# A two-layer hybrid decoder trunk: reciprocal roots of the norms on DVE alone, and the norm weights applied where the high and low parts are made

## The reference

```python
def rmsnorm(x, g):
    xf = x.astype(jnp.float32)
    y = xf * lax.rsqrt(jnp.mean(xf * xf, axis=-1, keepdims=True) + EPS)
    return (y * g.astype(jnp.float32)).astype(x.dtype)

def reference(x, mem, ...):
    for l in range(DEPTH):
        h = rmsnorm(x, norm_mix[l])
        qa, ka, va, qb, kb, vb, qi, ki, wi, qc, kc, vc, g = _split(h @ w_in[l], IN_SIZES)
        o_a = stick_breaking_attention(...)
        o_b = dsa_attention(rmsnorm(qb, qn_dsa[l]), rmsnorm(kb, kn_dsa[l]), vb, ...)   # top 64 keys
        o_c = sliding_window_attention(rmsnorm(qc, qn_swa[l]), rmsnorm(kc, kn_swa[l]), vc, ...)
        gates = jax.nn.sigmoid(g + b_gate[l])
        merged = gates[0] * (o_a @ w_pa[l]) + gates[1] * (o_b @ w_pb[l]) + gates[2] * (o_c @ w_pc[l])
        x = x + merged @ w_out[l]
        x = x + cross_attention(rmsnorm(x, norm_x[l]), rmsnorm(mem, norm_mem[l]), ...)
        hf = rmsnorm(x, norm_ffn[l])
        if l % 2 == 0:
            x = x + swiglu(hf, w_gu_dense[l // 2], w_down_dense[l // 2])
        else:
            x = x + moe_swiglu(hf, w_router[l // 2], w_gu_moe[l // 2], w_down_moe[l // 2])   # 2 of 8 experts
    return x
```

## Time and profile before

| what | value |
|---|---|
| time, median of 3 runs | 1813.37 us (1812.16 to 1819.61) |
| the profiled execution's own time | 1814.6 us |
| its span | 1813.0 us |
| mean granted PE clock | 0.984 of full |
| PE busy | 1717.1 us (95%) |
| DVE busy | 1405.6 us (78%) |
| ACT busy | 1112.3 us (61%) |
| POOL busy | 93.7 us (5%) |

### The profile page before, as it was taken

How to read it: one execution, slowest core, us unless ns; L and a number is a source line. 1 busy time by engine, 2 the same in 40 slices (tenths; PEclk the granted TensorE clock), 3 DMA queues, 4 the chain that set the end, 5 groups by cost and what they waited for, 6 DMA issues and landing times.

```text
span 1813.0 us, 22257 instructions
## 1 busy us (share of the span) xinstructions
PE 1717.1 (95%) x7776; PEld 1373.4 (76%) x7776; DVE 1405.6 (78%) x1258; ACT 1112.3 (61%) x1006; POOL 93.7 (5%) x68
## 2 busy tenths in 40 slices
PE   6999887999989998879999989999999999999999
PEld 5877666788768676667888878888788888788776
DVE  5798675554477967748888878888888888888897
ACT  4646354444345453537777777777777777877765
POOL 1200000000003000010000000000000000000440
PEclk9999998999999999979999999999999999999999
DMA  8533592555445325409999989999999999999985
GB/s 288 206 107 135 189 349 93 186 184 185 162 140 204 134 104 186 186 22 397 365 361 380 366 314 387 364 380 368 346 390 362 369 387 366 367 362 366 402 328 203
DMA packets 73791, 498.13 MB, mean 275 GB/s; under 512 B 8192, under 2 KB 8960, under 8 KB 17552
## 3 DMA queue, kind: packets, MB, share of 16 engines
q1 hardware_dynamic: 66000, 466.55, 67.9%
q0 software_dynamic: 7328, 29.87, 4.6%
q10 hardware_dynamic: 416, 1.08, 0.2%
HBM read 481.73 MB, written 15.73 MB: 274 GB/s over the span
## 4 chain that ended last, share of the span: by engine, by line
PE 77%; DVE 11%; ACT 4%; issue 3%; DVEq 3%; DMA 2%; ACTq 0%; SPq 0%; POOLq 0%
PE ps L516 24%; PE ps L520 24%; PE ps L512 24%; DVE w_lo L397 3%; DVE w_lo L901 1%; ACT w_hi L392 1%; PE ps L701 1%; DMA raw<-in_layer_tiles 1%; PE ps L1201 1%; DVE hT_lo L505 1%; DVE st L1447 1%; ACT w_hi L831 1%; DVEq L1450 1%; ACT scratch L1366 0%; DMA z<-rows_of_experts 0%
## 5 line engine op out<-in xcount | busy, mean ns | idle before, releaser
L512 PE MATMUL ps<-w_hi,hT_hi 128*128 128x512 f32 (+1 forms) x1552 | 436.5, 404 | 33.6 <-ACT hT_hi L500 10.6
L901 DVE TENSOR_TENSOR w_lo<-raw,w_hi 128x2048 fp32r<-128x2048 f32 x168 | 391.3, 2331 | 64.2 <-ACT w_hi L831 64.2
L901 DVE TENSOR_TENSOR w_lo<-z,w_hi 128x2048 fp32r<-128x2048 f32 x168 | 386.6, 2305 | 57.1 <-ACT w_hi L831 56.1
L516 PE MATMUL ps<-w_hi,hT_lo 128*128 128x512 f32 (+1 forms) x1552 | 424.3, 396 | 0.8 <-DVE hT_lo L505 0.4
L520 PE MATMUL ps<-w_lo,hT_hi 128*128 128x512 f32 (+1 forms) x1552 | 422.2, 394 | 0.7 <-DVE w_lo L397 0.7
L512 PEld LDWEIGHTS ps<-w_hi,hT_hi 128*128 128x128 f32 x1552 | 278.8, 190 | 96.7 <-ACT hT_hi L500 12.5
L516 PEld LDWEIGHTS ps<-w_hi,hT_lo 128*128 128x128 f32 x1552 | 290.9, 189 | 73.0 <-DVE hT_lo L505 4.1
L831 ACT ACTIVATE w_hi<-z 128x2048 fp32r<-128x2048 f32 x168 | 321.3, 1915 | 39.9 <-PE ps L520 36.2
L520 PEld LDWEIGHTS ps<-w_lo,hT_hi 128*128 128x128 f32 x1552 | 291.0, 189 | 71.2 <-DVE w_lo L397 1.6
L831 ACT ACTIVATE w_hi<-raw 128x2048 fp32r<-128x2048 f32 x168 | 321.1, 1912 | 25.5 <-PE ps L520 25.5
L397 DVE TENSOR_TENSOR w_lo<-raw,w_hi 128x2048 fp32r<-128x2048 f32 (+2 forms) x111 | 243.5, 2203 | 105.0 <-ACT w_hi L392 104.5
(11 more groups left out here) (260 smaller groups left out, 977.5 us busy)
## 6 DMA issues: line engine op xcount, KB each, us to landing
z<-in_moe_tiles SPq DMA_DIRECT2D x168, 1024.0 KB, 6.5
raw<-in_moe_tiles SPq DMA_DIRECT2D x168, 1024.0 KB, 6.5
raw<-in_layer_tiles SPq DMA_DIRECT2D x68, 1024.0 KB, 4.9
raw<-in_dense_tiles SPq DMA_DIRECT2D x33, 1024.0 KB, 4.8
rows_of_experts<-z POOLq DMA_DIRECT2D x1, 8704.0 KB, 37.8
raw<-in_layer_tiles SPq DMA_DIRECT2D x8, 512.0 KB, 3.6
z<-rows_of_experts POOLq DMA_DIRECT2D x8, 512.0 KB, 10.2
rows_of_experts<-z POOLq DMA_DIRECT2D x7, 512.0 KB, 8.1
```

Source lines behind the costliest of these rows:

```text
L512: pe.matmul(acc, hi[:, k, cols], wh, start=start and j == 0, stop=False)
L516: pe.matmul(acc, lo[:, k, cols], wh, start=False, stop=False)
L901: v.tensor_tensor(w_lo[:, ring, :], moe_raw(p), w_hi[:, ring, :].bitcast(F32), ALU.subtract) \
```

## The change

It has two parts. First, each reciprocal root is computed on DVE alone (`dve_rsqrt`): the bits of v are shifted right by one and subtracted from 0x5f3759df as integers, which gives a first value, and three Newton steps of three operations follow. With `v.drain()` between dependent operations that is 13 operations. `act_rsqrt`, `dve_var` and `dve_newton` go, and the roots stand where the variance stood (at the last norm, ahead of the row multiply by the weight).

Second, the multiply by the weight goes (`dve_gain`). ACT applies it while it makes the high part, chunk by chunk, since the weight is a scale column for each of eight chunks of 128x256 (`act_hi_gain`), and DVE while it subtracts (`dve_lo_gain`, one scalar_tensor_tensor for each chunk). Both read PSUM. The memory's low part moves from POOL to DVE. PE's waits on `mix_F` and `mem_F` become waits on `mix_L` and `mem_L`. The router's weights are scaled a little later in layer 1, and one `w_lo` of the cross attention moves behind the row maxima.

```diff
-        def act_rsqrt(act, name, l):
-            c, k = rs_cols(name), RS_AT[name, l]
-            act.wait_ge(sem("var"), k + 1)
-            act.activation(tmp[:, c], var[:, c], ACT.Ln)
-            act.drain()
-            act.activation(rstd[:, c], tmp[:, c], ACT.Exp, scale=-0.5).then_inc(sem("rs0"), 1)
-        def dve_var(v, name, width):
+        def dve_rsqrt(v, name, width, dst=None):
             c = rs_cols(name)
             v.drain()
-            v.tensor_scalar(var[:, c], ss[:, c], 1.0 / width, EPS, ALU.mult, ALU.add).then_inc(sem("var"), 1)
-        def dve_newton(v, name, l, dst=None):
...
+            v.tensor_scalar(var[:, c], ss[:, c], 1.0 / width, EPS, ALU.mult, ALU.add)
+            v.drain()
+            v.tensor_scalar(tmp[:, c].bitcast(I32), var[:, c].bitcast(I32), 1, None, ALU.logical_shift_right)
+            v.tensor_scalar(half[:, c], var[:, c], -0.5, None, ALU.mult)
+            v.drain()
+            v.tensor_scalar(rstd[:, c].bitcast(I32), tmp[:, c].bitcast(I32), -1, 0x5f3759df, ALU.mult, ALU.add)
+            for n in range(3):
+                v.drain()
+                v.tensor_tensor(tmp[:, c], rstd[:, c], rstd[:, c], ALU.mult)
+                v.drain()
+                v.tensor_tensor(tmp[:, c], tmp[:, c], half[:, c], ALU.mult)
+                v.drain()
+                ins = v.scalar_tensor_tensor(rstd[:, c] if dst is None or n < 2 else dst, tmp[:, c], 1.5, rstd[:, c],
+                                             ALU.add, ALU.mult)
+            return ins
...
+        def act_hi_gain(act, name, l, dst):
             for i, ks in halves():
-                v.wait_ge(sem(name + "_T"), 2 * l + i + 1)
-                g = gains[:, g0 + ks.start:g0 + ks.stop].unsqueeze(2)
-                v.tensor_tensor(dst[:, ks, :], psT[:, ks, :], bc(g, [P, KC // 2, S]), ALU.mult) \
-                    .then_inc(sem(name + "_F"), 1)
+                act.wait_ge(sem(name + "_T"), 2 * l + i + 1)
+                for k in range(ks.start, ks.stop):
+                    ins = act.activation(dst[:, k, :], psT[:, k, :], ACT.Copy, scale=gain_of(name, l, k))
+                ins.then_inc(sem(name + "_H"), 1)
+
+        def dve_lo_gain(v, name, l, hi, dst):
+            for i, ks in halves():
+                v.wait_ge(sem(name + "_H"), 2 * l + i + 1)
+                for k in range(ks.start, ks.stop):
+                    ins = v.scalar_tensor_tensor(dst[:, k, :], psT[:, k, :], gain_of(name, l, k), hi[:, k, :].bitcast(F32),
+                                                 ALU.mult, ALU.subtract)
+                ins.then_inc(sem(name + "_L"), 1)
...
@@ dve_program, layer start
-                dve_gain(v, "mix", l)
-                dve_split_to(v, cnt, s0 + 1)
-                dve_lo(v, "mix", l, hTf)
+                dve_lo_gain(v, "mix", l, hT_hi, hT_lo)
                 dve_split_to(v, cnt, s0 + 2)
                 for i in range(TT):
                     dve_sumsq(v, x_sb, i, 0)
-                dve_var(v, "mix", D)
+                dve_rsqrt(v, "mix", D, norm_rs[:, 0:2])
                 dve_split_to(v, cnt, s0 + RING)
-                dve_newton(v, "mix", l, norm_rs[:, 0:2])
...
                 dve_heads_var(v, l)
-                dve_gain(v, "mem", l, memT)
+                dve_lo_gain(v, "mem", l, o_hi, o_lo)
                 dve_linear(v, cnt, "in", l, take_in(v), s0 + 12, b0=2, b1=3)
...
@@ dve_cross
-            dve_var(v, "xq", P)
-            dve_split_to(v, cnt, end_of("xq", l) + 2)
-            dve_newton(v, "xq", l)
+            dve_rsqrt(v, "xq", P)
             v.drain()
```

More of the change, by code:

```diff
@@ L151, in build @@
         w_router = sb("w_router", [P, KC, N_EXP])
-        st = sb("st", [P, 192])
+        st = sb("st", [P, 224])
         n_iter = sb("n_iter", [1, 2], I32)
@@ L178, in build @@
         top_s8 = st[:, 184:192]
+        half = st[:, 192:224]
         def bc(ap, shape):
@@ L350, in add_window @@
             pool.drain().then_inc(sem("bias_ready"), 1)
[L352 to L356, removed]
         def pool_program(pool):
@@ L1044, in pe_heads @@
             pe.wait_ge(sem("heads_n"), l + 1)
-            pe.wait_ge(sem("mem_F"), 2 * l + 2)
+            pe.wait_ge(sem("mem_L"), 2 * l + 2)
             for j in range(8):
@@ L1216, in pe_program @@
                 pe.wait_ge(sem(f"mem{l}_in"), 16)
-                pe.wait_ge(sem("mix_F"), 2 * l + 2)
+                pe.wait_ge(sem("mix_L"), 2 * l + 2)
                 pe_turn(pe, "mem", mem_n)
@@ L1361, in act_cross @@
                 .then_inc(sem("x_qT"), 1)
-            act_rsqrt(act, "xq", l)
             for g in range(8):
@@ L1382, in act_program @@
                 act_split_to(act, cnt, s0 + (1 if l == 0 else RING))
[L1383 to L1386 removed]
                 if l == 0:
[L1388 removed]
+                    act.wait_ge(sem("gains"), 16)
+                act_hi_gain(act, "mix", l, hT_hi)
                 act_split_to(act, cnt, s0 + 6)
@@ L1400, in act_program @@
                 act_hi(act, "mrg", l, psT, "mrg_T", mm=end_of("pc", l))
-                act_rsqrt(act, "xk", l)
                 act_split_to(act, cnt, end_of("out", l) + 2)
-                act_hi(act, "x", l, hTf, "x_F", mm=end_of("out", l))
+                act_hi_gain(act, "x", l, hT_hi)
                 act.wait_ge(sem("x_keys_T"), l + 1)
@@ L1475, in dve_heads_var @@
             v.tensor_reduce(ss[:, 0:30], squares.rearrange("p (h d) -> p h d", d=HD), AX.X, ALU.add)
-            dve_var(v, "heads", HD)
+            dve_rsqrt(v, "heads", HD)
         def dve_heads(v, l):
@@ L1638, in dve_cross_keys_ss @@
             v.tensor_reduce(ss[:, 0:8], sq.rearrange("p (h d) -> p h d", d=P), AX.X, ALU.add)
-            dve_var(v, "xk", P)
+            dve_rsqrt(v, "xk", P)
         def dve_cross_keys(v, l):
@@ L1673, in dve_cross @@
                     .then_inc(sem("x_max"), 1)
+            dve_split_to(v, cnt, end_of("xq", l) + 1)
             for i, g in enumerate(tiles):
@@ L1801, in dve_program @@
                         dve_sumsq(v, mem_n, i, 30)
-                    dve_var(v, "mem", D)
+                    dve_rsqrt(v, "mem", D, norm_rs[:, 2:4])
+                else:
+                    g0 = (GAIN["ffn"] * L + L - 1) * KC
+                    v.wait_ge(sem("router_in"), 16)
+                    v.tensor_tensor(w_router[:, :, :], w_router[:, :, :],
+                                    bc(gains[:, g0:g0 + KC].unsqueeze(2), [P, KC, N_EXP]), ALU.mult) \
+                        .then_inc(sem("w_router_g"), 1)
                 dve_linear(v, cnt, "in", l, take_in(v), gate0[l], b0=1, b1=2)
-                if l == 0:
-                    dve_newton(v, "mem", l, norm_rs[:, 2:4])
                 dve_heads_var(v, l)
-                dve_gain(v, "mem", l, memT)
+                dve_lo_gain(v, "mem", l, o_hi, o_lo)
                 dve_linear(v, cnt, "in", l, take_in(v), s0 + 12, b0=2, b1=3)
@@ L1822, in dve_program @@
                 dve_hT(v, "x", l)
+                dve_rsqrt(v, "x", D, norm_rs[:, 4:6])
                 dve_split_to(v, cnt, blocks["xq", l] + RING)
-                dve_newton(v, "x", l, norm_rs[:, 4:6])
                 v.drain()
```

50 lines of the change are left out of this document (10 added, 40 removed).

## The result

| | kernel before | changed kernel |
|---|---|---|
| time, median | 1814.65 us (1812.16 to 1819.61, 7 runs) | 1826.26 us (1823.93 to 1831.89, 7 runs) |
| ratio to before | 1 | 1.0065, interval 1.0048 to 1.0083 |
| span of the profiled execution | 1813.0 us | 1823.7 us |
| mean granted clock | 0.984 | 0.978 |

The change makes the kernel slower by 0.65%, 11.8 us by the ratio and 11.6 by the medians. The forecast was 1829, its range 1820 to 1835. It was added to 1813.37, the median of three; the median of seven lies 1.3 higher.

The account below looks back on a forecast made before the run. The prediction took TensorE (PE), busy for 95% of the span, as the bound, so only its gaps count. Terms summed to +9.5 us, with the clock +15.5, added to the 1813.37 median: 1829, range 1820 to 1835.

Parts of the forecast that it names:

- Prices: Small drained DVE operations 0.23 to 0.24 us apart, integer taken as float; eight low products 3.3 us, eight high halves 3.1.
- In projection: Between blocks 2 and 3, both layers: root and eight products on DVE delay the evacuation PE needs, +3.6 us each.
- Layer 0's start: Low halves and root on DVE move the evacuation from 31.90 to 35.6, PE's next block near 36.4: +3.6 us.
- Start of layer 1: Evacuation stays near 522.38 and PE, starting the block earlier, waits about 4 us for it: +0.2 us.
- To the out projection: Stage ahead of out projection: xk's root -0.9 us per layer, layer 0's short wait -0.3, layer 1's mixers +1.3.
- Mixers: Layer 1: one more table load ahead of the first Exp, on the chain to PE: +1.3 us.
- Router: The root now stands uncovered ahead of the row gain and the router's first copy: +2.8 us.
- x and xq: Per layer: x stage -0.3 us, x's root -0.7 with PE's wait falling from 1.59 to 0.9, xq's root -0.6.
- Clock, +6: Four new PE gaps, both starts and both block 3s, each lose 1.5 us at lower clock: 6.0, bounds 0 and 8.
- rival C: Cross attention keeps the full clock, 8.2 us less in all: +7.3, 1821 us, not slower beyond noise; chance 0.10.

Follow-up runs that it names:

- one move: Changed kernel with the memory's low half made behind block 2's evacuation instead of ahead of it, both layers; ratio to the kernel before 1.0008.
- the late router root: Changed kernel with the last root moved from ahead of the router's chain to behind the choice of experts; ratio to the kernel before 1.0059.
- the early root: Changed kernel with layer 0's first root in DVE's idle time and the first w_lo ahead of the turned rows' low half; ratio to before 1.0068.
- the kernel with POOL's low half: Changed kernel with the memory's low half made by POOL from a gained copy that ACT writes; ratio to the kernel before 1.0102.
- the same change in better order: Changed kernel with every move of order together, and block 0's evacuation ahead of the fourth w_lo; ratio to the kernel before 0.9977.

## Why the prediction was right, point by point

The sign and the size held: +11.8 measured, +15.5 forecast, with its largest terms where it put them. In the trace the changed kernel is 14.0 behind where the experts begin, and the three largest errors of the forecast partly cancel there, which is luck: 1.5 too little for the in projections, 1.4 too much for layer 0's start, 2.7 too much for layer 0's cross attention.

**Right.** *Prices:* steps of 0.24 and 0.27, integer as float, eight products 3.22 (3.3), eight high halves 3.01 (3.1). *In projection:* 3.46 and 3.48 waited, 3.6 forecast; undone by one move. *Layer 0's start:* the evacuation at 35.65 (35.6), PE at 36.54 (36.4). *Start of layer 1:* +1.8, forecast 0.2 and 1.5 of clock, with the wait of 4.14 (about 4); three executions of the same instructions took 3.1. *To the out projection:* -1.1 and +0.5, forecast -1.2 and +0.4; the wait of 0.27 behind the turning of the heads is gone. *Mixers:* the new load took 1.28, and moving it took 0.9 out of the path there (1.3 forecast). *Router:* +3.0 (+2.8). *x and xq:* the wait 0.84 (0.9), and the 1.3 from x's and xq's roots measured 1.4 to 1.7 in the table's kernels with roots on DVE, and 0.0 to 0.1 in both with the old ones.

**Clock, +6: mis-sized place by place, about right in sum.** What PE's groups took above 0.93 each behind the four waits was 0, 1.5, 2.8 and 1.6 us, 5.9 in all. *In projection:* 6.4 and 5.3 in place of 5.1 each; the 2.8 is above the 2 that the prediction set as the most for one gap. *Layer 0's start:* forecast 3.6 and 1.5 behind it, 3.7 measured. In this execution PE was slow until 28.8 us, so block 0 ended late, the wait shrank to 0.78, and nothing was lost behind it. The prediction had the first w_lo at 23.5, but no slow clock around it. In other executions of the same instructions the two terms came as forecast. With the late router root the slow matmuls ended at the first w_lo (23.37), PE waited 3.43 for the evacuation and lost 2.7 behind it:

```profile
36.40 2.05 PE L510 MATMUL ps<-w_hi,hT_hi 128*128 128x512 f32 x4 [3.43 <-DVE z L567]
```

The forecast of 5.1 lies inside the 3.5 to 6.2 of the six executions.

**Cross attention, rival C.** The forecast had 6.35 us for the output products stay. In layer 0 it fell to 3.69, which gave 2.7, and in layer 1 it did not. Over the profiled executions the stage from the long wait to the xo projection took either 10.3 to 10.8 or 12.2 to 13.8 us. With the old roots it was the long one in 6 of 6 stretches, with roots on DVE in 9 of 22. So rival C was neither out nor the case: the shorter waits let the clock stay up in some executions. That the shorter chain is the cause is argued from this count, not shown.

**What the sum had not.** POOL's subtraction held up DVE. The prediction said that its going gives DVE room for a multiply behind the evacuation, which is hidden; it did not see that without its going, the longer roots would have driven the w_lo into it. For that reason, and because the new roots free ACT of the loads that hold up a w_hi, the change's two halves are not additive (12 and 5 apart, 12 together).

**Left open:** why the early root's 3 to 5 us don't show in its times; what makes the kernel with POOL's low half 7 us slower, of which the trace shows 2.1; and what decides, from one execution to the next, where the clock falls.

## What to carry over

An engine that is full in a stage has an order, and before a chain moves to it, ask which of its operations somebody waits for and put the others behind: here one call cost 10 of 12 us. Longer work on one engine also shifts what stands behind it into another engine's time, so look for operations whose duration already depends on a neighbour. And a root that needs no other engine can be moved to where its engine is idle: the same change in better order beat the kernel before by 4 us. No run makes the other moves in the kernel before, so how much of that is due to the change and how much to the order alone is not shown.

## What the hardware showed that I had not expected

- A small DVE operation can last as long as a POOL instruction beside it: 2.25 and 2.29 us for 30 columns, 0.19 alone; 6.65 for two w_lo, 4.49 alone.
- Behind waits of 3.42 to 3.48 us, in the same program, PE lost between 1.6 and 2.8 us at 1.2 GHz, and the output products took 3.69 or 6.63. Over all traces here, PE lost 1.2 to 2.9 us behind each of the 24 waits of 3.4 to 4.8 us ahead of an in-projection block; behind those of 1.8 to 3.0 us it lost 1.1 to 1.6 or nothing.
- Six to twelve runs of one kernel spread over 7 to 13 us, so an edit worth 1 to 3 us shows in its stage of a trace and not in its times.
- The two halves of a change can hide each other's costs: the waits of 4.77 and 2.45 us with one half each became 3.46 with both.
- Integer operations on DVE took 0.17 and 0.18 us at 2 and 30 columns, as float ones do.
